# A hybrid encoder layer on one core: squares of the norms in the tails of two projections, stick features one place ahead in the linear attention, memory queries read in place

## What is computed

```python
hn = rmsnorm(h, g_mix);  proj = hn @ w_in
o_gla = gla(q, k, v, log_alpha)          # 4 heads, chunks of 64, a state carried from chunk to chunk
o_sb  = stick_breaking(qs, ks, vs)       # 8 heads, needs its own features from hn @ w_in
h = h + concat(rmsnorm(o_gla) * silu(og), o_sb) @ w_out
h = h + mem_xattn(rmsnorm(h), rmsnorm(mem), w_q, w_kv, w_o)   # softmax over 256 memory tokens
h = h + peer(rmsnorm(h), ...)            # 128 experts' rows a token, gathered from memory
out = rmsnorm(h)
```

## Time and profile before

| | |
|---|---|
| median of 3 runs | 3706.51 us (3705.04 to 3707.81) |
| the profiled execution | 3705.7 us, its span 3703.9 us |
| mean granted TensorE clock | 0.912 of full speed |
| busy share of the span | PE 78%, PEld 39%, DVE 69%, ACT 41%, POOL 41% |
| DMA busy share, first 11 of 40 slices | 0 to 3 tenths |
| DMA busy share, last 29 of 40 slices | 9 tenths or more, about 410 GB/s |

### The profile page before, as it was taken

How to read it: one execution, slowest core, us unless ns; L and a number is a source line. 1 busy time by engine, 2 the same in 40 slices (tenths; PEclk the granted TensorE clock), 3 DMA queues, 4 the chain that set the end, 5 groups by cost and what they waited for, 6 DMA issues and landing times.

```text
span 3703.9 us, 32338 instructions
## 1 busy us (share of the span) xinstructions
PE 2896.9 (78%) x8696; PEld 1456.9 (39%) x8696; DVE 2554.9 (69%) x5661; ACT 1501.5 (41%) x3958; POOL 1518.9 (41%) x1176
## 2 busy tenths in 40 slices
PE   6999999787978788777877888776766666766666
PEld 5777544676823233333333333322222222222222
DVE  3453454534467887888778877877787788778776
ACT  3221596322233534554344433344343434434342
POOL 0000111000055544555445545555556655556654
PEclk8999999898989899989999999888889888888988
DMA  2101002212299999999999999999999999999998
GB/s 80 41 23 46 1 1 103 84 65 68 69 392 418 418 414 417 405 411 419 411 415 409 416 409 416 403 410 416 413 410 420 413 408 420 413 417 413 413 418 345
DMA packets 177612, 1155.95 MB, mean 312 GB/s; under 512 B 19984, under 2 KB 22048, under 8 KB 46240
## 3 DMA queue, kind: packets, MB, share of 16 engines
q0 software_dynamic: 147456, 1073.81, 70.5%
q1 hardware_dynamic: 29984, 80.26, 6.2%
HBM read 1149.80 MB, written 4.19 MB: 312 GB/s over the span
## 4 chain that ended last, share of the span: by engine, by line
DMA 39%; PE 11%; ACT 8%; issue 7%; DVE 5%; POOL 2%; POOLq 0%; DVEq 0%; ACTq 0%
DMA expert_rows<-in_uv,choice_index 39%; PE expert_acc L2166 11%; DVE expert_rows L1940 2%; ACT L2042 2%; POOL expert_rows L1774 2%; ACT L1360 2%; DVE expert_own_acc L1914 1%; ACT expert_wt L2044 1%; ACT expert_dg L2053 1%; ACT expert_wt L2042 1%; ACT choice_best L1360 1%; PE expert_side L2092 0%; ACT L1991 0%; DVE expert_dot L1940 0%; ACT expert_spare L1991 0%
## 5 line engine op out<-in xcount | busy, mean ns | idle before, releaser
L2166 PE MATMUL expert_acc<-expert_rows,expert_dg 128*128 128x512 f32 x3072 | 1689.8, 689 | 670.6 <-ACT expert_dg L2053 667.4
L1774 POOL DMA_INDIRECT expert_rows<-in_uv,choice_index x1024 | 1469.3, 1435 | 1295.1 <-PE expert_acc L2166 737.5
L1940 DVE CUSTOM_DVE_ANT_0 expert_rows<-expert_rows,expert_xn 128x1024 f32<-128x1024 f32 x1024 | 1251.9, 1223 | 560.7 <-DMA expert_rows<-in_uv,choice_index 554.8
L2166 PEld LDWEIGHTS expert_acc<-expert_rows,expert_dg 128*128 128x128 f32 x3072 | 615.5, 215 | 1685.5 <-ACT expert_dg L2053 1116.7
L2042 ACT ACTIVATE expert_wt<-expert_dot 128x1 f32<-128x1 f32 x1024 | 207.5, 203 | 1486.6 <-DVE expert_dot L1940 1485.7
L1914 DVE SCALAR_TENSOR_TENSOR expert_own_acc<-expert_rows,expert_wt,expert_own_acc 128x1024 f32<-128x1024 f32 x248 | 317.7, 1281 | 3.5 <-ACT expert_wt L2044 3.5
L2053 ACT ACTIVATE expert_dg<-ident,expert_wt 128x128 f32<-128x128 f32 x768 | 308.4, 402 | 25.2
L2044 ACT ACTIVATE expert_wt<-expert_wt,choice_gate 128x1 f32<-128x1 f32 x1024 | 301.4, 294 | 33.4
L2077 PE MATMUL expert_side<-expert_w_raw,mix_b 128*128 128x512 f32 x256 | 128.7, 605 | 0.0
L1060 POOL TENSOR_SCALAR_AFFINE_SELECT heads<-heads 128x128 f32<-128x128 f32 x64 | 20.7, 323 | 262.8 <-DVE heads L1124 262.6
L2092 PE MATMUL expert_side<-z_b,expert_w_raw 128*128 128x512 f32 x256 | 126.2, 595 | 0.0
(11 more groups left out here) (356 smaller groups left out, 3684.4 us busy)
## 6 DMA issues: line engine op xcount, KB each, us to landing
expert_rows<-in_uv,choice_index POOLq DMA_INDIRECT x1024, 12.2
H<-in_x SPq DMA_DIRECT2D x8, 1024.0 KB, 10.2
pq_w_raw<-in_w_pq SPq DMA_DIRECT2D x16, 512.0 KB, 3.6
expert_w_raw<-in_w_pq SPq DMA_DIRECT2D x32, 256.0 KB, 8.9
stick_w_raw<-in_w_feat SPq DMA_DIRECT2D x8, 512.0 KB, 3.6
tok_w_raw<-in_w_tok SPq DMA_DIRECT2D x8, 512.0 KB, 3.8
out_w_raw<-in_w_out SPq DMA_DIRECT2D x8, 512.0 KB, 6.4
mk_w_raw<-in_w_mk SPq DMA_DIRECT2D x8, 512.0 KB, 3.6
```

The costliest lines, as they stand in the source:

```text
L1774: pool.indirect_dma_start(out=rows[R % ROWS], out_offset=None, in_=uv, in_offset=bass.IndirectOffsetOnAxis(ap=index[:, q, r:r + 1], axis=0 ...
L1940: nc.vector.tensor_tensor_reduce(rows[R % ROWS][:, 0:D], rows[R % ROWS][:, 0:D], xn[:, :], 1.0, 0.0, ALU.mult, ALU.add, dot[:, h % 2, r:r ...
L2166: last_mm = nc.tensor.matmul(acc[:, h * HALF:(h + 1) * HALF], dg[:, n % DG, :], rows[R % ROWS][:, D + h * HALF:D + (h + 1) * HALF], start= ...
```

## The change

It has three parts. First, `token_gemm_phase` takes a list of blocks, and ScalarE computes their sums of squares after its last `highs`, each as soon as VectorE has finished the block (the two memory blocks as soon as they have landed); `memnorms` and `ffnnorm` are given these sums and leave out their own squares, on both engines. Second, in the linear attention each half of the stick features moves one place ahead in TensorE's order; VectorE's copies move with them, and TensorE's loop is written out. Third, the memory attention's scores read the query tile `q_a` directly; the copy to `mem_qb` and its semaphore are gone, and the scores of block b + 2 wait for the exponentials of block b instead.

```diff
@@ norm_phase @@
-            for b in range(0, nb, 2):
+            for b in range(0, 0 if sums else nb, 2):
-            for b in range(1, nb, 2):
+            for b in range(1, 0 if sums else nb, 2):
@@ token_gemm_phase, ACT, behind its highs @@
+            if squares:
+                link = Chain(act, squared)
+                for b in range(first, nb + before):
+                    if b < before:
+                        act.wait_ge(extra, 16 * len(loads))
+                    else:
+                        act.wait_ge(bank_free, nb * n_chunks + b - before + 1)
+                    link(nc.scalar.activation(junk[:, :], tok(b), ACT.Square, accum_out=ms[:, b:b + 1]))
@@ gla_phase, DVE @@
             def attend(b, s):
                 link.restart()
+                empty(b, 0)
                 dve.wait_ge(scores, b + 1)
...
                 dve.sem_inc(masked, 1)
-                empty(b, 0)
+                empty(b, 1)
                 for c in range(NC):
-                    if c:
-                        empty(b, 1)
                     dve.wait_ge(sums, 2 * b + c + 1)
@@ gla_phase, PE @@
-            with pe.Fori(0, NB // 2) as i:
-                for s in range(2):
-                    b = 2 * i + s
+            half(0, 0, 0)
+            for b in range(NB):
+                s = b % 2
...
                 last.then_inc(turned, 1)
-                    half(b, s, 0)
+                half(b, s, 1)
                 pe.wait_ge(masked, b + 1)
...
-                        if c:
-                            half(b, s, 1)
+                    if c and b + 1 < NB:
+                        half(b + 1, 1 - s, 0)
                     wait_alone(co, pe, state_ready, 2 * b + c + 1)
@@ memory_attention_phase @@
-            def queries(b, s):
-                act.wait_ge(s_full, b + 1)
-                nc.scalar.activation(qb[:, s, :, :], q_t[:, :, ds(b * P, P)], ACT.Copy).then_inc(q_ready, 1)
...
             def attend(b, s):
-                pe.wait_ge(q_ready, b + 1)
+                if b >= 2:
+                    pe.wait_ge(probs, MEM_HEADS * (b - 1))
...
-                        last = nc.tensor.matmul(ps[s][:, h, :], qb[:, s, HD * h + k, :], k_t[:, HD * h + k, :],
+                        last = nc.tensor.matmul(ps[s][:, h, :], q_t[:, HD * h + k, b * P:(b + 1) * P], k_t[:, HD * h + k, :],
@@ program @@
+        sums_q, sums_f = co.sb("sums_q", [P, MB + NB // 2]), co.sb("sums_f", [P, NB // 2])
-            token_gemm_phase(co, "mixout", by_tokens(x_t), NB // 2, w_out, add, loads=loads + more)
+            tok_q = lambda b: m_tok[:, b, :] if b < MB else co.H[:, b - MB, :]
+            token_gemm_phase(co, "mixout", by_tokens(x_t), NB // 2, w_out, add, loads=loads + more, squares=(tok_q, sums_q, 0, MB))
-                token_gemm_phase(co, "memout", by_tokens(y_t), NB // 2, w_mo, add)
+                token_gemm_phase(co, "memout", by_tokens(y_t), NB // 2, w_mo, add,
+                                 squares=(lambda b: co.H[:, b, :], sums_f, 0, 0))
```

More of the change, by code:

```diff
@@ L181, in rstd_steps, with norm_phase @@
         link(nc.vector.tensor_tensor(y, y, t, ALU.mult))
-def norm_phase(co, name, tok, nb, gain, place, rstd, loads=()):
+def norm_phase(co, name, tok, nb, gain, place, rstd, loads=(), sums=None):
     nc = co.nc
@@ L197, in norm_phase @@
     with ExitStack() as cx:
-        ms = co.sb(f"{name}_ms", [P, nb], ctx=cx)
+        ms = sums or co.sb(f"{name}_ms", [P, nb], ctx=cx)
         var = co.sb(f"{name}_var", [P, nb], ctx=cx)
@@ L416, in feature_gemm_phase, with token_gemm_phase @@
     co.end_phase()
-def token_gemm_phase(co, name, x, nb, w, evac, loads=()):
+def token_gemm_phase(co, name, x, nb, w, evac, loads=(), squares=None):
     nc = co.nc
@@ L433, in token_gemm_phase @@
         banks = [cx.enter_context(nc.psum_tensor(f"{name}_bank{j}", [P, HALF], F32)) for j in range(nb)]
+        if squares:
+            tok, ms, first, before = squares
+            squared = co.sem(f"{name}_squared")
+            junk = cx.enter_context(nc.psum_tensor(f"{name}_junk", [P, D], F32))
         block = cx.enter_context(nc.Block())
@@ L816, in _ @@
             pe.sem_inc(half_full, 2 * HALVES)
-            with pe.Fori(0, NB // 2) as i:
-                for s in range(2):
-                    b = 2 * i + s
-                    wait_alone(co, pe, operands, b + 1)
+            half(0, 0, 0)
+            for b in range(NB):
+                s = b % 2
+                wait_alone(co, pe, operands, b + 1)
+                for h in range(2):
+                    feats = slice(h * CHUNK, (h + 1) * CHUNK)
+                    for a in range(2):
+                        for c in range(NC):
+                            for u in range(NSUB):
+                                last = nc.tensor.matmul(
+                                    pa[h][c * CHUNK:(c + 1) * CHUNK, a, u * SUB:(u + 1) * SUB],
+                                    kh[feats, s, a, c, u, :],
+                                    qh[feats, s, a, c * CHUNK + u * SUB:c * CHUNK + (u + 1) * SUB],
+                                    start=True, stop=True)
+                last.then_inc(scores, 1)
+                for a in range(2):
+                    last = nc.tensor.transpose(pk[:, a * P:(a + 1) * P], kd[:, s, a, :], co.ident[:, :])
+                last.then_inc(turned, 1)
+                half(b, s, 1)
+                pe.wait_ge(masked, b + 1)
+                pe.wait_ge(values, b + 1)
+                pe.wait_ge(o_free, 2 * b + 2)
+                for h in range(2):
+                    for a in range(2):
+                        nc.tensor.matmul(po[h][:, a, :], at[:, s, 2 * a + h, :],
+                                         vb[:, s, (2 * a + h) * GLA_DV:(2 * a + h + 1) * GLA_DV],
+                                         start=(a == 0), stop=False, skip_group_check=True)
+                for c in range(NC):
+                    rows = slice(c * CHUNK, (c + 1) * CHUNK)
+                    if c and b + 1 < NB:
+                        half(b + 1, 1 - s, 0)
+                    wait_alone(co, pe, state_ready, 2 * b + c + 1)
                     for h in range(2):
@@ L824, in _ @@
                         for a in range(2):
[L825 to L835, removed]
-                    half(b, s, 0)
-                    pe.wait_ge(masked, b + 1)
-                    pe.wait_ge(values, b + 1)
-                    pe.wait_ge(o_free, 2 * b + 2)
+                            last = nc.tensor.matmul(po[h][rows, a, :], qi[feats, s, a, rows], state[feats, c, a, :],
+                                                    start=False, stop=(c == NC - 1), skip_group_check=True)
@@ L840, in _ @@
+                    if c == NC - 1:
+                        last.then_inc(o_full, 1)
+                    if c == 0:
+                        wait_alone(co, pe, turned_sb, b + 1)
                     for h in range(2):
+                        feats = slice(h * CHUNK, (h + 1) * CHUNK)
                         for a in range(2):
-                            nc.tensor.matmul(po[h][:, a, :], at[:, s, 2 * a + h, :],
-                                             vb[:, s, (2 * a + h) * GLA_DV:(2 * a + h + 1) * GLA_DV],
-                                             start=(a == 0), stop=False, skip_group_check=True)
@@ L845, in _ @@
-                    for c in range(NC):
-                        rows = slice(c * CHUNK, (c + 1) * CHUNK)
-                        if c:
-                            half(b, s, 1)
[L849 to L867, removed]
@@ L868, in gla_phase @@
+                            hd = 2 * a + h
+                            last = nc.tensor.matmul(pst[c][feats, a, :], kt[rows, s, hd * GLA_DK:(hd + 1) * GLA_DK],
+                                                    vb[rows, s, hd * GLA_DV:(hd + 1) * GLA_DV], start=True, stop=True)
+                    last.then_inc(sums, 1)
     co.end_phase()
@@ L1199, in memory_attention_phase @@
     sem = lambda n: co.sem(f"mem_{n}")
-    q_ready, s_full, max_ready, probs, normed, turned, turned_sb, o_full, o_taken = (
-        sem(n) for n in ("q_ready", "s_full", "max_ready", "probs", "normed", "turned", "turned_sb", "o_full", "o_taken"))
+    s_full, max_ready, probs, normed, turned, turned_sb, o_full, o_taken = (
+        sem(n) for n in ("s_full", "max_ready", "probs", "normed", "turned", "turned_sb", "o_full", "o_taken"))
     done = sem("done")
@@ L1239, in body @@
                 if more:
-                    queries(b + 2, s)
                     exps(b + 2, s)
-            for b in range(2):
-                queries(b, b)
             for b in range(2):
@@ L2298, in program @@
             w_pq = pieces("pq_w", 2 * PH, 1, a['w_pq'], cx, raw_slots=2).ahead()
-            norm_phase(co, "ffnnorm", lambda b: co.H[:, b, :], NB // 2, lambda b: gains[:, 3, :], by_block(z_a), rstd[:, 0:NB // 2])
+            norm_phase(co, "ffnnorm", lambda b: co.H[:, b, :], NB // 2, lambda b: gains[:, 3, :], by_block(z_a), rstd[:, 0:NB // 2], sums=sums_f)
```

7 lines of the change are left out of this document (4 added, 3 removed).

## The result

| | before | after |
|---|---|---|
| median | 3706.32 us (4 runs) | 3736.60 us (4 runs) |
| profiled execution, its span | 3705.7, 3703.9 us | 3736.52, 3734.8 us |
| mean granted clock | 0.912 | 0.913 |

The change makes the kernel slower by 30.3 us: a ratio of 1.0078, 95% interval 1.0066 to 1.0091. The forecast was 3735.0 with a range of 3718 to 3745.

The account below looks back on a forecast made before the run. Ahead of a fixed 2674 us row-gathering stage, phases run one after another, so their changes move everything: linear attention +41.2, memory attention -9.6, norms -3.1, sum +28.5 us, forecast 3735.0, range 3718 to 3745.

Parts of the forecast that it names:

- The new wait: Linear attention: TensorE idles about 6.5 us before half(b, 1), until VectorE's copy behind operand(b+1); seven times.
- The period: Linear attention, middle block: 23.06 us against 17.92, +5.14 a block; about 25 us with the lower clock.
- The clock's term: Linear attention: after each idle TensorE restarts at the lower clock, costing 2.0 us a block, ends 0 and 2.5.
- First and last block: Linear attention: block 0 loses 2.9 us, its masked product at 174.6 instead of 171.65; block 7 gains 4.5.
- The memory attention: Without the query copy, first scores start 1.0 us earlier and block 2's wait shrinks: -9.6 us, ends -7.1 and -3.1.
- The other stride of the query tile: Memory attention: scores read the query tile at another stride than `mem_qb`; bounded at 1.5 us either way, taken as 0.
- The norms: Both norms: variance 3.8 us after the last addition began, against 5.92 and 4.75: -2.1 and -1.0, together -3.1 us.
- the clock holds: Rival in the linear attention: the wait comes but TensorE stays at the high level; +14.5, 3721 us; chance 0.20 wholly or partly.
- The new wait doesn't bite: Rival at TensorE before half(b, 1): empty(b, 0) done before the scores end; -27, 3680 us; chance 0.05.

Follow-up runs that it names:

- The early copy: Changed kernel, but VectorE copies half (b+1, 0) between its two state updates, and half (0, 0) between operand(0) and operand(1): 3685.92 us.
- the second bank: Changed kernel with two half banks taking turns in the linear attention, the transposes sharing a bank with the first key-value sums: 3692.92 us.
- the run with fillers: Changed kernel with 44 additional matmuls, results overwritten, behind the transposes of each of blocks 0 to 6 in the linear attention: 3722.26 us.
- the run without the loads: Kernel before with the norms' part of the change alone, and without the explicit table load ahead of the two norms: 3702.42 us.
- the version with the copy early and the low part late: The early copy's kernel, with VectorE's low part of weight tile b + 1 moved from ahead of the masks of block b to behind them: 3680.89 us.

## Why the prediction was right, step by step

- **The new wait.** Right in place and kind: seven waits, ended by the copy L721, 41.1 us in all, 5.9 each and 6.1 the longest, where I had said about 6.5. The rows gave less than I said: the half can start 8.37 us into the block and the transposes end 2.20 us into it (218.16 + 0.44 - 216.40), so 6.2; the sum didn't use the 6.5. The early copy and the second bank both remove it.
- **The period.** I summed 23.06 us for a middle block at the high clock and 25.06 with the clock's term. The changed kernel shows 24.95 ((334.58 - 184.88) / 6), between 24.3 and 25.7 from block to block, and the run with fillers 22.95 without the clock's term.
- **The clock's term.** 2.0 us a block, taken from the half in the first block of the kernel before: 24.95 - 22.95 = 2.0 measured, and 14.3 us in all where I had 14. The Trainium skill ("TensorE: Matmul & The Clock Gate", section "HAM oscillation") describes a loop whose engine waits for a transfer in each round and starts each round at the lower clock. The trace agrees, with a wait for VectorE in its place: the clock is at 0.50 around the start of the half in each of the seven blocks, as from 241 to 243 us above.
- **First and last block.** The first masked product came at 175.90 instead of 171.65, of which 0.9 lies ahead of the phase: +3.35 where I had +2.9. The last block took 11.84 instead of 16.44: -4.6 against -4.5. In sum the linear attention took 41.85 - 0.9 = 40.95 us more (last state update at 346.42 instead of 304.57); I had 41.2.
- **The memory attention.** From VectorE's last copy of the queries (L406) to the start of the next projection: -10.0 in the trace (52.39 to 42.41), -9.7 in its own run, -9.6 forecast. The start gave 0.8, not 1.0; the wait of block 2 and its clock gave 6.9, not 6.5. The other stride of the query tile, which I had taken as 0, shows no cost: the first scores took 7.14 us against 7.17.
- **The norms.** 5.92 to 3.69 and 4.75 to 3.68 us: -2.2 and -1.1 against -2.1 and -1.0. That the gain is small because the last square and the load stand bare was right, and so was the load without a drain behind it: the variance on VectorE began 0.04 us after the load's end (715.24 + 1.28, 716.56). The Trainium skill ("ScalarE: Activation LUTs", section "What ACT_TABLE_LOAD costs") gives its drain for a switch to a different set. Here the set was there already, since the run without the loads has no other load in their place, so this load is no such switch and the trace doesn't speak against the page.
- **What was off.** The parts in the trace sum to 40.95 - 10.0 - 3.3 = +27.7, while the gathers began 31.2 later. The other 3.5 us lie in stages that the change doesn't touch: 0.9 before the linear attention, 1.4 between the memory norms and the memory attention, the rest in the projection and scores behind it. Differences of this size are also within what one kernel shows from run to run: the kernel before lay between 3703.86 and 3709.72 us in 26 runs. I took the untouched stages as fixed; that they are not, by 1 us or so each, is the term that I left out. What sets it wasn't tried. The granted clock's changes fall at other points of these stages in each run, which would do it; that is argued, not shown.

The rivals: "the clock holds" (3721) is what the fillers brought about by force, 3722.3, and isn't what the changed kernel does. "The new wait doesn't bite" (3680) is nearly the version with the copy early and the low part late, 3680.9: the price of that rival was right, its condition false.

## What to carry to other kernels

When work is moved up on one engine, look at who frees its buffer, and at what stands ahead of that on its own queue: the copy of 0.69 us was no later in the program's text than its use, but it came behind 7.5 us of VectorE's other work and waits. Move the release with the use; here it fitted into a wait that VectorE had anyway. And the wait on TensorE was dearer than it was long: of the 7.0 us that a middle block lost (24.95 against 17.92), 2.0 were the lower clock of the work behind it.

## What the runs showed of the hardware

In the memory attention an idle of TensorE of 3.21 us was followed by the low level (0.50 from 812 to 814 us), while idles of 1.50, 2.06 and 2.29 us in the same phase of the kernel before left the clock at 1.00. The length of one idle doesn't settle it, though: in the run with two banks the clock fell to 0.66 between 190 and 195 us behind a wait of 1.68 us, and stayed at 1.00 behind the like waits of five other blocks. What makes the difference wasn't tried. That 44 matmuls whose results are thrown away can make a kernel 14 us faster I had expected by the sum, but hadn't seen: each block bought 2.0 us with them. And an explicit table load of a set that is already there took its full 1.28 us on ScalarE at both norms of the changed kernel.
